# Loading the meta tokens turned: sixteen four-byte-element transfers in place of sixteen TensorE transposes

## The chip, the core and the metric

One core of one Trainium2 chip runs the whole program. The metric is the device time of one execution in microseconds. Before the change it is 2454.93 us (median of three runs, 2454.27 to 2454.93).

## What is computed

The program takes x (256 tokens by D = 2048 features, fp32) through two blocks. The first is an attention block and a squared-ReLU MLP. The second puts 16 learned meta tokens ahead of the 256 tokens, so its first products run over 272 columns:

```python
meta = jnp.broadcast_to(meta_tokens[None].astype(x.dtype), (b, N_META, D_MODEL))   # (1, 16, 2048)
h = jnp.concatenate([meta, x], axis=1)
hn = rms_norm_2(h, norm_mix_g)       # x * rsqrt(mean(x*x)) * gain, per token
proj = hn @ w_in                     # columns of the pool, the convolution and the gates
```

Pool and convolution look back over up to 15 tokens, which is why the meta tokens matter. They are left out again at the end: `return out[:, N_META:]`.

## The kernel before, in words

**Layout.** Activations stand turned: features on the 128 partitions, 16 tiles of 128 features (NT = 16), tokens along the free axis. `a_buf` has 272 columns a tile: 16 for the meta tokens, 256 for x.

**Weights.** All weights are fp32 in HBM and come in chunks of 512 rows by 512 columns (1 MB), over 450 of them. A chunk goes into one of four `raw` buffers by one transfer on SyncE's queue (SP, line 548), which waits until VectorE has split the chunk that stood there. ScalarE rounds each half of a chunk (a unit, [128, 2, 512]) to `whi` (line 602), VectorE takes the rest into `wlo` (line 810), and TensorE multiplies whi by the high and low part of the activations (line 1365 or 1420) and wlo by the high part (line 1372 or 1428). There are four unit buffers of whi and wlo, that is two chunks: ScalarE fills one as soon as TensorE has done with it.

**Stages.** A list of stages is run by every engine in the same order. `q` is chunks 0 to 15, `kv` 16 to 47, `w_o` 48 to 63, and `w1_0`, the first panel stage of the MLP, chunks 64 to 79; then come `w2_0`, `w1_1`, `w2_1`, ..., `w1_3`, `w2_3`, then `u`, the first stage that reads the meta columns. Stages of one iteration are unrolled. Each engine's order is what its `body` writes out: ScalarE's splits a chunk two ahead, then does whatever is written for this chunk, then the evacuation of a panel when its last chunk is at hand.

**Meta tokens.** SyncE loads `meta_tok` ([16, 2048], line 526) behind eight small vectors. In stage q, after chunk (1, 1), TensorE turns it by `meta_turn` (line 1340): sixteen transposes into spare columns of PSUM bank 6. VectorE's `meta_operand` copies them to U (line 882), multiplies by the gain of the norm into `meta_f` (line 884), squares (line 888) and reduces to `msum` (line 890). `meta_f` is a view of the tile rr1, and `msum` of rr, so the trace names them rr1 and rr. Behind stage w1_3 ScalarE's `meta_high` rounds meta_f into the meta columns of a_buf (line 770) and VectorE's `meta_low` takes the rest (line 896). VectorE's `z_out`, in the attention, waits for the reduction, since its tile t2 lies over U.

**The end.** TensorE's last products of the output are those of `last_chunks` (lines 1530 and 1535). VectorE and ScalarE then add, square, scale and store the two halves of the tokens. After `run`, TensorE has 42 products more, called `spare` (line 1605), that nothing reads.

Of the kernel before, what the change touches and what calls it, by code (L numbers as in the profile page):

```python
# [15 lines left out]
ALU = mybir.AluOpType  # L16
# [4 lines left out]
P = 128  # L21
D = 2048
NT = D // P
T = 256
MT = T // P
M = 16
# [235 lines left out]
def build(nc, x, meta, norm_mix, norm_mlp, final_norm, w_qkv, w_o1, w1, w2, norm_mix_2, w_in, b_gate,  # L262
# [6 lines left out]
    with ExitStack() as ctx:  # L269
# [13 lines left out]
        def sem(name):  # L283
            return ctx.enter_context(nc.semaphore(name))
# [46 lines left out]
        sqt = S2[:, :, 0:T]  # L331

        x_tok, _ = place("x_tok", [P, MT, D], at=region)
        meta_tok, _ = place("meta_tok", [M, D], at=region + 16384)
        x_sq, _ = place("x_sq", [P, MT, D], at=b_off)
        gm, _ = place("gm", [NT, P], at=region + 24576 + 1536)
        gv, _ = place("gv", [96, 2, P], at=region + 24576)
# [46 lines left out]
        vec_t = sem("vec_t")  # L384
        vec_ready = sem("vec_ready")
        tr_done = sem("tr_done")
        meta_t = sem("meta_t")
        meta_step = sem("meta_step")
        meta_hi = sem("meta_hi")
        norm_mm = sem("norm_mm")  # L390
# [110 lines left out]
        def _(sp):  # L501
# [16 lines left out]
            def load_vectors():  # L518

                for v, r0 in ((norm_mix[0], V_MIX), (norm_mlp[0], V_MLP), (final_norm, V_FIN1), (norm_mix_2, V_MIX2), (norm_ffn_2, V_FFN2),  # L520
                              (pool_scale, V_PS)):
                    sp.dma_start(gv[r0:r0 + NT, 0, :], v.rearrange("(t p) -> t p", p=P)).then_inc(vec_landed, 16)
                sp.dma_start(gv[0:2 * NT, 1, :], b_gate.rearrange("(t p) -> t p", p=P)).then_inc(vec_landed, 16)
                sp.dma_start(gv[2 * NT:5 * NT, 1, :], conv_w.rearrange("k (t p) -> (k t) p", p=P)
                             ).then_inc(vec_landed, 16)
                sp.dma_start(meta_tok[:], meta).then_inc(meta_landed, 16)

            load_x(0)

# [58 lines left out]
        def _(act):  # L588
            cnt = Counts()
            act.dma_start(gm[:], norm_mix[0].rearrange("(t p) -> t p", p=P)).then_inc(mix_landed, 16)  # L590

            def split_hi(ahead=AHEAD // UNITS):

# [136 lines left out]
            def body(st, i):  # L730
                for q, (k, c) in enumerate(st.order):
                    p = st.panels[k]
                    first = st.name == "q" and k == 0
                    if not first and not split_early[0]:
                        split_hi()
                    split_early[0] = False
                    cnt.n["chunk"] += 1
                    if st.norm is not None and k == 0 and c == NORM_CHUNK:
                        root(st.norm)
                    if st.name == "dn_2" and k == 3 and c == 0:  # L740

                        act.activation(ms[:, 1, 0:2], ms[:, 0, 0:2], ACT.Sqrt)
                    if st.name == "dn_0" and (k, c) in H_TURNS:
                        h_out(H_TURNS.index((k, c)))
                    for g, step in attn_steps(st, q):
                        if step == 7:
                            weights_hi(g)
                    if c == p.chunks - 1:
                        cross_out(p, k % 2)
                        if attn_over(st, q):  # L750

                            split_hi()
                            split_early[0] = True
                        evac(p, k // 2 if p.kind in ("k", "v") else st.index(i, k))
                        cnt.closed(p)
                    for g, step in attn_steps(st, q):
                        if step == 2:
                            softplus_ln(g)
                        if step == 4:
                            softplus_hi(g)  # L760
                        if step == 6:
                            weights_exp(g)
                        if step == 8:
                            evac(ATTN, g)
                            cnt.event("attn")
# [25 lines left out]
        def _(dve):  # L791
# [85 lines left out]

            def meta_operand():

                meta_raw = U[:, 0, 0:NT * M]  # L880
                dve.wait_ge(meta_t, 1)
                dve.tensor_copy(meta_raw, ps[:, 6, T:T + NT * M]).then_inc(meta_step, 1)
                dve.wait_ge(meta_step, 1)
                dve.tensor_tensor(meta_f, meta_raw.rearrange("p (t n) -> p t n", n=M),
                                  vec[:, V_MIX2:V_MIX2 + NT].unsqueeze(2).to_broadcast([P, NT, M]),
                                  ALU.mult).then_inc(meta_step, 1)
                dve.wait_ge(meta_step, 2)
                dve.tensor_tensor(U[:, 1, 0:NT * M], meta_raw, meta_raw, ALU.mult).then_inc(meta_step, 1)
                dve.wait_ge(meta_step, 3)
                dve.tensor_reduce(msum, U[:, 1, 0:NT * M].rearrange("p (t n) -> p n t", n=M), mybir.AxisListType.X,  # L890
                                  ALU.add).then_inc(meta_step, 1)

            def meta_low():

                dve.wait_ge(meta_hi, 1)
                dve.tensor_tensor(a_lo[:, :, 0:M], meta_f, cast(a_hi[:, :, 0:M]), ALU.subtract).then_inc(meta_step, 1)

            def z_out(g):

                dve.wait_ge(z_ready, g + 1)  # L900
                dve.wait_ge(meta_step, 4)
                if g > 0:
                    dve.wait_ge(aw_lo, g)
                for b, hd in ((2, 0), (6, 2)):
# [244 lines left out]
            def body(st, i):  # L1149
                for q, (k, c) in enumerate(st.order):  # L1150
# [9 lines left out]
                    cnt.n["chunk"] += 1  # L1160
                    if st.name == "q" and k == 1 and c == 2:
                        vectors()
                        meta_operand()
                    if st.norm is not None and k == 0 and c == NORM_CHUNK:
                        norm(st.norm)
                    if p.kind == "last" and c == 0:
# [131 lines left out]
        def _(pe):  # L1298
# [28 lines left out]
            def vectors():  # L1327

                pe.wait_ge(vec_landed, 16 * 8)
                pe.wait_ge(diag_ready, 2)  # L1330
                for b, v0, v1 in ((0, 0, V_BG), (1, V_BG, V_END)):
                    last = pe.transpose(ps[:, 7, T + v0:T + v1], gv[0:v1 - v0, b, :], ident[0:v1 - v0, 0:v1 - v0])
                last.then_inc(vec_t, 1)

            def meta_turn():

                pe.wait_ge(meta_landed, 16)
                pe.wait_ge(x_out, PIECES)
                for t in range(NT):
                    last = pe.transpose(ps[:, 6, T + t * M:T + (t + 1) * M], meta_tok[:, t * P:(t + 1) * P],  # L1340
                                        ident[0:M, 0:M])
                last.then_inc(meta_t, 1)

            def token_rows():

# [147 lines left out]
            def norm(k):  # L1493

                pe.wait_ge(sums_ready, k + 1)
                last = pe.matmul(ps[:, 7, 0:T], ones[:], acc[:, 0, :], start=True, stop=True, skip_group_check=True)
                if k == 1:
                    pe.wait_ge(meta_step, 5)
                    pe.matmul(ps[:, 6, 0:M], ones[:], msum, start=True, stop=True, skip_group_check=True)
                    last = pe.matmul(ps[:, 6, M:TW], ones[:], acc2[:, 0, :], start=False, stop=True,  # L1500
                                     skip_group_check=True)
                last.then_inc(norm_mm, 1)
# [53 lines left out]
            def body(st, i):  # L1556
                for q, (k, c) in enumerate(st.order):
# [5 lines left out]
                    if c == 0:  # L1563
# [1 line left out]
                        if st.name == "q" and k == 1:  # L1565
                            pe.wait_ge(vec_ready, 1)
                        if st.name == "u" and k == 0:
                            pe.wait_ge(meta_step, 5)
                        if st.norm == 1 and k == 1:
                            pe.wait_ge(norm_mid, 3)  # L1570
                        elif st.norm is not None and k == 1:
# [6 lines left out]
                        token_rows()  # L1578
                    if st.name == "q" and k == 1 and c == 1:
                        vectors()  # L1580
                        meta_turn()
                    if st.name == "dn_0" and (k, c) in H_TURNS:
                        if (k, c) == H_TURNS[0]:
                            gated[0] = cnt.n["full"]
# [13 lines left out]

            run(pe, cnt, body)

            row = d_hi.rearrange("p t n -> p (t n)")

            def spare(i, stationary, moving, n):

                pe.matmul(ps[:, 2 + i % 2, 0:n], stationary, moving, start=True, stop=True, skip_group_check=True)  # L1605

            def block(i):

                return whi[:, i // 8, i // 4 % 2, i % 4 * P:(i % 4 + 1) * P]

            for i in range(6):
                spare(i, block(0), by_turns(d_hi[:, i, :]), T)
            for i in range(6):
                spare(i, block(i), by_turns(d_hi[:, i, 0:192]), 192)
            for i in range(6):
                spare(i, block(i), by_turns(d_hi[:, i, 0:P]), P)
            for i in range(6):
                spare(i, block(i), row[:, i * T:(i + 8) * T].rearrange("p (a n) -> p n a", a=2)[:, 0:P, :], T)
            for i in range(6):
                spare(i, block(i), d_hi[:, i, :].rearrange("p (a n) -> p n a", a=4), T)  # L1620
            for i in range(6):
                spare(i, block(i), d_hi[:, i, 0:1].to_broadcast([P, T]), T)
            for i in range(6):
                spare(i, b_hi[:, i, 0:P], by_turns(d_hi[:, i, :]), T)


# [21 lines left out]
```

## Time and profile before

| | |
|---|---|
| median of 3 runs | 2454.93 us (2454.27 to 2454.93) |
| the profiled execution's own time | 2454.94 us |
| its span, first to last instruction | 2453.2 us |
| TensorE busy | 2448.2 us |
| VectorE, ScalarE, GpSimd busy | 1652.5, 1206.5, 142.7 us |
| DMA | 485.34 MB, mean 198 GB/s |
| granted TensorE clock | 1.00 throughout |

The span is 1.7 us shorter than the time of the same execution; what lies around the span is not in the trace. Queue q1 is SyncE's, q10 ScalarE's. A packet is one contiguous run of a transfer, or the four-byte write of a semaphore at an engine's end of a transfer. A share of a queue is of 16 engines' time. The chain of work is followed back from the last instruction of an engine, which here isn't the last thing to happen: the stores land after it.

### The profile page before, as it was taken

What the parts mean: (1) busy time and instruction counts of PE and PEld (TensorE: products, weight loads), DVE (VectorE), ACT (ScalarE), POOL (GpSimd) and SP (SyncE); (2) the same over time, 40 slices, a digit from 0 to 9 for tenths busy, and PEclk for the clock granted to TensorE, in tenths of its full rate; (3) what the DMA queues carried; (4) which work ended last, traced back from release to release, by engine and by line L of the source; (5) the groups of instructions that cost most, each with busy time, mean ns of one, the idle gap of its engine ahead of it and who ended that gap; (6) DMA issues with size and microseconds to landing.
All of it is one profiled execution on the core that took longest, in us unless ns stands there. A gap on an engine that the chain in (4) does not pass through costs nothing.

```text
span 2453.2 us, 39643 instructions
## 1 busy us (share of the span) xinstructions
PE 2448.2 (100%) x15839; PEld 2273.1 (93%) x15839; DVE 1652.5 (67%) x1415; ACT 1206.5 (49%) x1185; POOL 142.7 (6%) x87
## 2 busy tenths in 40 slices
PE   9999999999999999999999999999999999999999
PEld 9999999999999999999999999999999889988998
DVE  7677777656656666787765886666766556665665
ACT  5456555444444444544543344544554544444444
POOL 0001100000000000000200630000000000000001
DMA  8655556666666666565656566666666565666664
GB/s 267 200 174 170 172 189 202 196 203 205 196 199 205 199 198 203 190 204 190 205 191 203 191 201 196 203 206 200 195 205 201 192 200 196 204 204 200 197 221 138
DMA packets 243960, 485.34 MB, mean 198 GB/s; under 512 B 7728, under 2 KB 8944, under 8 KB 243696
## 3 DMA queue, kind: packets, MB, share of 16 engines
q1 hardware_dynamic: 243520, 483.12, 59.9%
q8 instruction: 86, 1.41, 0.2%
q10 hardware_dynamic: 320, 0.53, 0.1%
q14 instruction: 34, 0.28, 0.0%
HBM read 481.53 MB, written 2.10 MB: 197 GB/s over the span
## 4 chain that ended last, share of the span: by engine, by line
PE 99%; DMA 0%; issue 0%; DVE 0%; SPq 0%; ACT 0%
PE ps L1365 44%; PE ps L1372 23%; PE ps L1420 12%; PE ps L1399 8%; PE ps L1428 6%; PE ps L1405 4%; PE ps L1476 0%; PE ps L1442 0%; PE ps L1530 0%; DMA raw<-in_sb_w_qkv_dram 0%; PE ps L1464 0%; PE ps L1605 0%; PE ps L1513 0%; PE ps L1535 0%; PE ps L1467 0%
## 5 line engine op out<-in xcount | busy, mean ns | idle before, releaser
L810 DVE TENSOR_TENSOR wlo<-raw,whi 128x1024 fp32r<-128x1024 f32 x900 | 1144.8, 1284 | 750.7 <-ACT whi L602 749.3
L602 ACT ACTIVATE whi<-raw 128x1024 fp32r<-128x1024 f32 x900 | 947.8, 1056 | 1154.1 <-PE ps L1372 815.7
L1365 PE MATMUL ps<-b_buf,whi 128*128 128x512 f32 x2816 | 666.3, 379 | 0.0
L1365 PEld LDWEIGHTS ps<-b_buf,whi 128*128 128x128 f32 x2816 | 506.3, 190 | 56.6
L1372 PEld LDWEIGHTS ps<-b_buf,wlo 128*128 128x128 f32 x2816 | 369.0, 191 | 18.9
L1372 PE MATMUL ps<-b_buf,wlo 128*128 128x256 f32 x2816 | 371.1, 275 | 0.0
L1365 PE MATMUL ps<-c_buf,whi 128*128 128x512 f32 x1280 | 303.0, 380 | 0.0
L1420 PE MATMUL ps<-a_buf,whi 128*128 128x258 f32 (+4 forms) x2304 | 282.2, 276 | 1.1 <-issue 1.1
L1420 PEld LDWEIGHTS ps<-a_buf,whi 128*128 128x128 f32 x2304 | 269.6, 191 | 1.6 <-issue 1.3
L1365 PEld LDWEIGHTS ps<-c_buf,whi 128*128 128x128 f32 x1280 | 230.1, 190 | 25.7
L1365 PE MATMUL ps<-a_buf,whi 128*128 128x512 f32 x896 | 211.9, 379 | 0.0
L1365 PEld LDWEIGHTS ps<-a_buf,whi 128*128 128x128 f32 x896 | 161.0, 190 | 18.0
L1372 PEld LDWEIGHTS ps<-c_buf,wlo 128*128 128x128 f32 x1280 | 167.8, 191 | 8.6
L1372 PE MATMUL ps<-c_buf,wlo 128*128 128x256 f32 x1280 | 168.7, 275 | 0.0
L1399 PE MATMUL ps<-whi,d_buf 128*128 128x512 f32 x672 | 159.1, 380 | 0.0
L1428 PE MATMUL ps<-a_buf,wlo 128*128 128x258 f32 (+4 forms) x1152 | 153.0, 276 | 0.1
L1399 PEld LDWEIGHTS ps<-whi,d_buf 128*128 128x128 f32 x672 | 126.5, 189 | 17.7
L1428 PEld LDWEIGHTS ps<-a_buf,wlo 128*128 128x128 f32 x1152 | 140.3, 191 | 0.4 <-DVE wlo L837 0.3
L1372 PEld LDWEIGHTS ps<-a_buf,wlo 128*128 128x128 f32 x896 | 117.4, 191 | 6.0
L1372 PE MATMUL ps<-a_buf,wlo 128*128 128x256 f32 x896 | 118.1, 275 | 0.0
L985 DVE TENSOR_TENSOR full<-ps,full 128x1024 f32<-128x1024 f32 x78 | 95.0, 1217 | 0.0
L1405 PE MATMUL ps<-wlo,d_buf 128*128 128x512 f32 x336 | 86.2, 379 | 0.0
(204 smaller groups left out, 1374.6 us busy)
## 6 DMA issues: line engine op xcount, KB each, us to landing
raw<-in_mlp_w_dram SPq DMA_DIRECT2D x128, 1024.0 KB, 5.2
raw<-in_w_in_dram SPq DMA_DIRECT2D x96, 1024.0 KB, 5.1
raw<-in_w_gate_up_dram SPq DMA_DIRECT2D x88, 1024.0 KB, 5.0
raw<-in_sb_w_qkv_dram SPq DMA_DIRECT2D x44, 1024.0 KB, 5.1
raw<-in_w_down_dram SPq DMA_DIRECT2D x44, 1024.0 KB, 5.1
raw<-in_sb_w_o_dram SPq DMA_DIRECT2D x16, 1024.0 KB, 5.2
raw<-in_conv_out_w_dram SPq DMA_DIRECT2D x16, 1024.0 KB, 5.1
raw<-in_w_o_dram SPq DMA_DIRECT2D x16, 1024.0 KB, 5.1
```

Of the source, the lines that this page charges most:

```text
L602: act.activation(whi[:, unit_of(n, u)], raw[:, n % RAW, u * UK:(u + 1) * UK, :], ACT.Copy).then_inc(w_hi, 1)
L810: dve.tensor_tensor(wlo[:, s], raw[:, n % RAW, u * UK:(u + 1) * UK, :], cast(whi[:, s]), ALU.subtract).then_inc(w_lo, 1)
L985: step(dve.tensor_tensor(in_halves(full[:]), turned(half, 0), in_halves(full[:]), ALU.add))
L1365: pe.matmul(ps[:, 4 * half + j, :].rearrange("p (c n a) -> p c n a", c=2, a=2), whi[:, unit_of(n, u), kt, j * P:(j + 1) * P], parts_by_tur ...
L1372: last = pe.matmul(ps[:, 4 * half + j, T:2 * T], wlo[:, unit_of(n, u), kt, j * P:(j + 1) * P], by_turns(buf[:, 0, p.tile0 + c * KT + u * U ...
L1399: pe.matmul(ps[:, 4 * half + m, :], part[:, x, toks[m]], by_turns(whi[:, s, kt, :]), start=first and kt == 0 and part is hi, stop=False, s ...
L1405: last = pe.matmul(ps[:, 4 * half + m, :], hi[:, x, toks[m]], by_turns(wlo[:, s, kt, :]), start=False, stop=stop and kt == UK - 1, skip_gr ...
L1420: pe.matmul(outs[j], whi[:, s, kt, j * P:(j + 1) * P], by_turns(part[:, x, tok]), start=first and kt == 0 and part is hi and (wide_ or j % ...
L1428: last = pe.matmul(outs[j], wlo[:, s, kt, j * P:(j + 1) * P], by_turns(hi[:, x, tok]), start=False, stop=stop and kt == UK - 1, skip_group ...
```

## The change

SyncE no longer loads meta_tok. In stage w1_0 ScalarE issues, once for each of the 16 chunks, a transfer that reads 128 features of the 16 meta tokens from HBM turned, straight into meta_f: 128 partitions by 16 elements, each element a run of four bytes of its own. TensorE's sixteen transposes and VectorE's copy out of PSUM are gone. VectorE's three other operations on them move from stage q to behind stage w1_3, right ahead of meta_low, and ScalarE's meta_high now waits for them there. z_out's wait goes. The wait for x_out moves from meta_turn into `vectors`. The 42 spare products are gone too.

```diff
-                sp.dma_start(meta_tok[:], meta).then_inc(meta_landed, 16)
@@ scalar
+            def load_meta(t):
+
+                act.dma_start(meta_f[:, t, :], meta[:, t * P:(t + 1) * P].rearrange("m p -> p m"),
+                              allow_slow_non_contiguous=True).then_inc(meta_landed, 16)
@@ scalar, body: behind split_hi() and the count of the chunk
+                    if st.name == "w1_0":
+                        load_meta(q)
@@ vector
             def meta_operand():
-                meta_raw = U[:, 0, 0:NT * M]
-                dve.wait_ge(meta_t, 1)
-                dve.tensor_copy(meta_raw, ps[:, 6, T:T + NT * M]).then_inc(meta_step, 1)
+                squares = U[:, 1, 0:NT * M]
+                dve.wait_ge(meta_landed, 16 * NT)
+                dve.tensor_tensor(squares, rr1[:], rr1[:], ALU.mult).then_inc(meta_step, 1)
                 dve.wait_ge(meta_step, 1)
-                dve.tensor_tensor(meta_f, meta_raw.rearrange("p (t n) -> p t n", n=M),
-                                  vec[:, V_MIX2:V_MIX2 + NT].unsqueeze(2).to_broadcast([P, NT, M]),
+                dve.tensor_tensor(meta_f, meta_f, vec[:, V_MIX2:V_MIX2 + NT].unsqueeze(2).to_broadcast([P, NT, M]),
                                   ALU.mult).then_inc(meta_step, 1)
-                dve.wait_ge(meta_step, 2)
-                dve.tensor_tensor(U[:, 1, 0:NT * M], meta_raw, meta_raw, ALU.mult).then_inc(meta_step, 1)
-                dve.wait_ge(meta_step, 3)
-                dve.tensor_reduce(msum, U[:, 1, 0:NT * M].rearrange("p (t n) -> p n t", n=M), mybir.AxisListType.X,
+                dve.tensor_reduce(msum, squares.rearrange("p (t n) -> p n t", n=M), mybir.AxisListType.X,
                                   ALU.add).then_inc(meta_step, 1)
             def meta_low():
+                meta_operand()
                 dve.wait_ge(meta_hi, 1)
@@ vector, z_out
-                dve.wait_ge(meta_step, 4)
@@ vector, body, stage q
                         vectors()
-                        meta_operand()
@@ tensor, vectors
+                pe.wait_ge(x_out, PIECES)
@@ tensor
-            def meta_turn():
-
-                pe.wait_ge(meta_landed, 16)
-                pe.wait_ge(x_out, PIECES)
-                for t in range(NT):
-                    last = pe.transpose(ps[:, 6, T + t * M:T + (t + 1) * M], meta_tok[:, t * P:(t + 1) * P],
-                                        ident[0:M, 0:M])
-                last.then_inc(meta_t, 1)
@@ tensor, behind run(pe, cnt, body): seven groups of six products into banks 2 and 3, all gone
-            for i in range(6):
-                spare(i, block(0), by_turns(d_hi[:, i, :]), T)
...
-            for i in range(6):
-                spare(i, b_hi[:, i, 0:P], by_turns(d_hi[:, i, :]), T)
```

In `norm` and ahead of stage u TensorE waits for meta_step 4 in place of 5, one step fewer having been made.

## Rows read from the trace of the kernel before

**Rows 1.** The page: the span, and busy time of each engine.
```profile
span 2453.2 us, 39643 instructions
PE 2448.2 (100%) x15839; PEld 2273.1 (93%) x15839; DVE 1652.5 (67%) x1415; ACT 1206.5 (49%) x1185; POOL 142.7 (6%) x87
```

**Rows 2.** Busy time in stretches: stage w1_0, w2_0, start, middle, end.
```profile
core 0: us, PE busy (x) PEld busy (x) DVE busy (x) ACT busy (x) POOL busy (x), PEclk, DMA share, GB/s
380.40:464.80 84.40, 84.40 (x517) 77.48 (x517) 61.40 (x54) 43.81 (x43) 1.84 (x2) 1.00 0.63 200
464.80:548.60 83.80, 83.80 (x514) 76.93 (x513) 50.50 (x43) 38.43 (x37) 0.00 (x0) 1.00 0.61 201
...
13.90:2446.00 2432.10, 2430.84 (x15721) 2256.68 (x15721) 1642.15 (x1400) 1197.82 (x1173) 140.93 (x77) 1.00 0.60 197
```

**Rows 3.** The chain in order of time, around the transposes: start, us, what.
```profile
43.22 0.89 PE ps L1428 x8
44.12 0.16 PE ps L1332 x2
44.27 1.09 PE ps L1340 x16
45.36 1.98 PE ps L1420 x16
47.34 0.89 PE ps L1428 x8
48.23 1.79 PE ps L1420 x16
```

**Rows 4.** Timeline of the end.
```profile
2446.00 4.37 PE L1605 MATMUL ps<-d_buf,whi 128*128 128x256 f32 x36
...
2448.67 0.75 DVE L1088 TENSOR_SCALAR y_tok<-y_tok,stat 128x1024 f32<-128x1024 f32 x1
...
2450.20 0.83 PE L1605 MATMUL ps<-d_buf,b_buf 128*128 128x256 f32 x6
```

**Rows 5.** What SyncE's own queue waited for, from 2435 us on.
```profile
SPq L269 <- DMA out_dram<-y_tok: 3.0, 1, 3.0
SPq L269 <- PEq L269: 0.2, 1, 0.2
```

**Rows 6.** DMA from 384 to 464 us: packets, queue, weight loads.
```profile
q1 hardware_dynamic: 7955, 15.80, 62.8%
raw<-in_mlp_w_dram SPq DMA_DIRECT2D x15, 1024.0 KB, 5.3
```

**Rows 7.** Queues from 2.5 to 5 us, then from 4 to 6 us.
```profile
q10 hardware_dynamic: 14, 0.00, 0.7%
...
q1 hardware_dynamic: 540, 0.65, 98.3%
```

**Rows 8.** Timelines: a weight load's issue, ScalarE's splits, TensorE's first products of w1_0.
```profile
356.88 5.61 SPq L548 DMA_DIRECT2D raw<-in_mlp_w_dram  x2
...
372.94 1.06 ACT L602 ACTIVATE whi<-raw 128x1024 fp32r<-128x1024 f32 x1 [1.62 <-PE ps L1372]
...
380.54 1.89 PE L1365 MATMUL ps<-c_buf,whi 128*128 128x512 f32 x8
```

**Rows 9.** Issue of a transfer: SyncE's of meta_tok, and line 548's on the weights.
```profile
15.69 0.42 SPq L526 DMA_DIRECT2D meta_tok<-in_meta_tokens_dram  x1
L548 SPq DMA_DIRECT2D raw<-in_mlp_w_dram x128: 367/373/393, 356.9 to 1025.7; - x128
```

**Rows 10.** Timeline of VectorE in stage q.
```profile
53.55 0.42 DVE L882 COPY U<-ps 128x256 f32<-128x256 f32 x1
54.01 0.42 DVE L884 TENSOR_TENSOR rr<-U,vec 128x256 f32<-128x256 f32 x1
54.47 0.43 DVE L888 TENSOR_TENSOR U<-U 128x256 f32<-128x256 f32 x1
54.93 0.59 DVE L890 TENSOR_REDUCE rr<-U 128x16 f32<-128x256 f32 x1
```

**Rows 11.** Timeline behind stage w1_3.
```profile
975.20 0.40 ACT L770 ACTIVATE a_buf<-rr 128x256 fp32r<-128x256 f32 x1
...
976.21 1.22 DVE L1110 TENSOR_TENSOR b_buf<-full,b_buf 128x1024 f32 x1
```

More of the change, by code:

```diff
@@ L333, in build @@
         x_tok, _ = place("x_tok", [P, MT, D], at=region)
-        meta_tok, _ = place("meta_tok", [M, D], at=region + 16384)
         x_sq, _ = place("x_sq", [P, MT, D], at=b_off)
@@ L386, in build @@
         tr_done = sem("tr_done")
-        meta_t = sem("meta_t")
         meta_step = sem("meta_step")
@@ L1497, in norm @@
                 if k == 1:
-                    pe.wait_ge(meta_step, 5)
+                    pe.wait_ge(meta_step, 4)
                     pe.matmul(ps[:, 6, 0:M], ones[:], msum, start=True, stop=True, skip_group_check=True)
@@ L1567, in body @@
                         if st.name == "u" and k == 0:
-                            pe.wait_ge(meta_step, 5)
+                            pe.wait_ge(meta_step, 4)
                         if st.norm == 1 and k == 1:
@@ L1580, in body @@
                         vectors()
-                        meta_turn()
                     if st.name == "dn_0" and (k, c) in H_TURNS:
@@ L1599, in _ @@
             run(pe, cnt, body)
[L1601 to L1609, printed above, removed]
-            for i in range(6):
-                spare(i, block(0), by_turns(d_hi[:, i, :]), T)
-            for i in range(6):
[L1614 to L1623, printed above, removed]
-                spare(i, b_hi[:, i, 0:P], by_turns(d_hi[:, i, :]), T)
 _INS = ["x", "meta_tokens_2", "norm_mix", "norm_mlp", "final_norm", "sb_w_qkv", "sb_w_o", "mlp_w1", "mlp_w2",
```

## The prediction, made before the changed kernel was run

> **What bounds the kernel now.** I read the page's busy times first: TensorE is busy for 2448.2 of 2453.2 us, the next engine, VectorE, for 1652.5 [rows 1]. The table of stretches then shows that nearly all of the missing time lies outside the middle: from 13.9 to 2446.0 us TensorE is busy for 2430.84 of 2432.10 us, at full clock, and in the two MLP stages that the change touches first it isn't idle at all [rows 2]. So TensorE sets the time between the first chunk and the last, and whatever another engine or a transfer does counts only where it makes TensorE wait. The chain of waits in order of time shows what one step of it costs; the end I read from the timeline and from SyncE's waits, because there the chain of the page follows the wrong thing (below).
>
> **TensorE loses sixteen transposes.** They stand on the chain itself, 1.09 us from 44.27 to 45.36, with no wait ahead or behind [rows 3]. The next sixteen products take 1.98 us where the same ones later take 1.79 [rows 3]; that 0.19 us comes with the change of product and may stay, because the two transposes of the vectors remain ahead of them. So the gain here is 1.09 to 1.28 us. I take 1.2. It is passed on to the end: the weights are split for TensorE well ahead of need (worked out below), so nothing is late next. The wait for x_out that moves into `vectors` is for copies of the first panel, whose results the products of that panel have used; TensorE reaches it three chunks later, at 44 us: nothing.
>
> **TensorE loses 42 products at the end.** They run from 2446.00 to 2451.03 [rows 4]. But the last scaling of the output ends at 2448.67 + 0.75 = 2449.42 [rows 4], its store is issued after it, and SyncE then waits 3.0 us for the stores to land, and only 0.2 us for TensorE's queue [rows 5]. With 0.4 us for the issue, 2449.8 + 3.0 is 2452.8, which is later than 2451.03 by 1.8 us and leaves the span's end at 2453.2. The products lie beside the tail, so I cost them at nothing. If that cover were gone, the price would be at most what they last, 4.9 us.
>
> **VectorE.** One copy (0.42 us) goes, and three operations of 0.43, 0.42 and 0.59 us move [rows 10]. They leave a stage where TensorE waited for nothing, so their going gives nothing. Behind w1_3 they are new work on a path: ScalarE's meta_high ran at 975.20, because its operand had been ready since 54 us, while VectorE took the low part of the last panel from 976.21 to 977.43 [rows 11]. Now meta_high must wait for that, for the squares and for the product with the gain: 977.43 + 0.43 + 0.42 + some 0.1 = 978.4 us, and it ends at 978.8. The split that is queued behind it on ScalarE came at 975.91 in the trace and now comes 2.9 us later. VectorE's own split, queued behind meta_operand and meta_low, ends about 2.2 us later. TensorE needs that split's unit three units on. A unit is half of a chunk, and the second stretch has 16 chunks in 83.80 us, so a chunk is 5.24 us and a unit 2.62 [rows 2]. ScalarE's split takes 1.06 us [rows 8], so it has 3 x 2.62 - 1.06 = 6.8 us to spare. 2.9 us fit in, and are made up within three units. Cost: nothing; if ScalarE had no such lead it would be 2.9 us.
>
> **ScalarE issues sixteen transfers.** The trace has an issue at 0.42 us for a small pattern and at 0.37 for a full 1 MB load [rows 9], so the number of packets doesn't show in it. ScalarE is busy for 43.81 us of the 84.40 of w1_0 [rows 2], 2.7 of each chunk's 5.24 us; 0.42 more leaves 2.1 us idle. One issue stands ahead of the norm's root at chunk 2 and delays it by at most 0.4 us; TensorE has the rest of the panel until it needs the scale's work. SyncE loses one issue of 0.42 us and 128 KB of traffic at a time when no weight is late: nothing. What could cost here is an issue that doesn't return until its packets are taken; that is a rival.
>
> **The transfers themselves** are the one term that could be large. Each has 128 x 16 = 2048 runs of four bytes: on each of 16 engines 128 packets and one for the semaphore, 129. The stage's own load: 7955 packets took 62.8% of 16 engines for 80 us, which is 101 ns a packet; a 1 MB chunk is 33 packets an engine, 3.3 us in every 5.24 [rows 6]. So 1.9 us a chunk are free on every engine. The trace of before has no read of four bytes. Its nearest row from below is the ScalarE queue at the start, where 14 packets of 512 bytes or of four (semaphores) took 0.7% of 16 engines for 2.5 us: 20 ns each [rows 7]. Its next is the stretch from 4 to 6 us, mostly runs of 1 KB: 540 packets in 98.3% of 32 us, 58 ns [rows 7]. The far end is the 101 ns of the 2 KB packets. I take 20 ns, since a four-byte packet is nearest to that row in size and the three rows fall with size. It gives 129 x 20 = 2.6 us a chunk, which is 0.7 more than is free. Served ahead of the weights throughout, that makes them late by 16 x 0.7 = 11 us at the end of the stage. Against it stands a lead: the load of chunk 64 is issued at 356.88 and lands 5.3 us later, at 362.2, and ScalarE first reads it at 372.94, so 10.8 us to spare; with the 6.8 of the split buffers, TensorE doesn't see a weight that is up to 17.6 us late [rows 6, 8]. 11 is less than 17.6: hidden, and with 0 ns a packet all the more. The landing itself has 500 us until it is needed.
>
> **The sum.** Against the profiled execution: 2454.94 - 1.2 = 2453.7 us, of which 2452.0 would be its span. That execution stands 0.01 us from the median, so the forecast for the median is 2453.7 too. No measurement of this kernel tells a change under 0.2% (4.9 us) from none with safety, so this is "within 0.2%".
>
> **Rivals.**
> (a) *The small packets are served in runs ahead of the weights, and each costs more than I take.* Engine time is then simply added. The stage's lateness is 16 x (129c - 1.9 us), and TensorE sees what passes 17.6 us: it decides from c = 23 ns on, little above what I take. At 58 ns: 16 x (7.5 - 1.9) = 89, less 17.6, is 72 us, 2526 us; at 101 ns 2614. For it: a run of four bytes has a read in HBM of its own, and no row shows one. Against it: packet time falls with size in all rows. Of the Trainium skill, "DMA: Bandwidth & Descriptors", section "Queues, rings and completion order", states that an engine changes between queues only after a whole group of typically 9 to 17 descriptors; by that rule this is how the queues would share, where one for one would be rival (b). The trace has no stretch in which both queues are full, so it doesn't show which. The same page's "Rules for kernel authors" says that turning data by a rearranged access pattern is a bad way to do it, 19 times slower than the transposing transfer; no row here bears on that factor, and it would speak for (a).
> (b) *The queues take turns packet by packet, and a four-byte packet costs as much as a weight's.* Weights then go at 101 + c ns a packet until the 16 x 129 = 2064 small ones of an engine are through. In that time 2064 / 33 = 62.5 chunks pass, which TensorE would use up in 328 us; with the lead of 17.6 it decides from c = 66 ns on. At 101 ns: 2064 x 0.202 = 417, less 345, is 72 us, 2526 us again. It needs a packet at the far bound.
> (c) *The issue blocks ScalarE until its transfer is taken.* Were each as long as a weight load's landing, 5.3 us, ScalarE would need 2.7 + 5.3 = 8.0 us a chunk for 5.24: 16 x 2.8 = 44, less its lead of 6.8, is 38 us, 2493 us. It decides from an issue of about 2.95 us on. Against it: 0.37 us for a load of 512 packets [rows 9].
> (d) *The change doesn't gain what it removes*: the time of the transposes is taken by a wait of TensorE's at that place or later. 2454.9 us. Against it: ScalarE's and VectorE's leads.
> (e) *The 42 products do set the end*, their modelled ends being too early. At most 4.9 + 1.2 less: 2448.8 us. Against it: SyncE's 3.0 us of waiting for the store.
>
> **How the numbers follow.** Hidden as forecast 0.69, (d) 0.06, (a) 0.11, (b) 0.07, (c) 0.05, (e) 0.02. The two first are within 0.2%: same 0.75. (a), (b) and (c) are slower: 0.23, save that each starts small beyond its threshold. (e) is faster: 0.02. The range goes from 2452.6 (1.28 us of gain, and half a microsecond and more of the runs' own scatter with a little of the tail) to 2463, which takes in (d) and the part of (a) to (c) just above their thresholds, c up to 27 ns in (a) (16 x 129 x 4 ns = 8 us), some 0.05. About 0.2 is left out, almost all of it above.
>
> **What would show it.** In the profile after: TensorE's products follow the two transposes of the vectors directly, and TensorE has no idle time from 380 to 560 us that the weights end. ScalarE's queue should have some 33,000 packets at about 20 ns; a share of q10 above 3 us a chunk, or weight loads of w1_0 that land in more than 15 us, would mean (a) or (b), and then VectorE's and ScalarE's idle time would end with a transfer. An issue above 1 us on ScalarE's queue would mean (c). TensorE should be idle in the last 7 us while the span's end stays 7 us behind the last product. meta_high should come 3 us later, with no gap on TensorE. The prediction is wrong if a four-byte packet costs more than 23 ns and is served first.

## The result, and the profile after

The changed kernel takes 2515.97 us (median of six runs, 2508.30 to 2520.47) against 2454.93 us before: a ratio of 1.0247, 95% interval 1.0237 to 1.0258. The forecast was 2453.7 us and no measurable change; the range ended at 2463. The profiled execution took 2513.46 us, its span is 2511.7, 58.5 us more than before.

The page of the changed kernel, its first parts (compare [rows 1]; the slices of the clock and of the GB/s are 63 us each):

```profile
span 2511.7 us, 39538 instructions
PE 2459.5 (98%) x15781; PEld 2276.5 (91%) x15781; DVE 1651.9 (66%) x1414; ACT 1204.7 (48%) x1185; POOL 142.4 (6%) x87
PEclk9999999889999999999999999999999999999999
GB/s 270 201 168 168 184 185 128 118 163 200 200 201 202 199 202 199 199 188 199 200 201 201 187 199 201 201 201 201 201 201 200 197 200 199 200 201 206 201 217 137
q10 hardware_dynamic: 33344, 0.66, 0.7%
```

TensorE has 58 fewer products and is busy for 11 us more. The rate drops in slices 7 to 9 (377 to 565 us), which hold stage w1_0 and the start of w2_0, and the clock stands at 8 tenths in slices 8 and 9. ScalarE's queue has the 33,000 packets foreseen, and they took even less than foreseen by the record: 0.7% of 16 engines for 2511.7 us is about 8.4 ns each. By that number alone they would be free.

Stretches of the changed kernel, the same columns as in [rows 2]:

```profile
440.00:460.00 20.00, 9.82 (x45) 8.26 (x44) 4.75 (x4) 4.92 (x5) 0.00 (x0) 0.76 0.42 113
...
380.00:560.00 180.00, 138.29 (x737) 120.65 (x736) 84.59 (x73) 59.31 (x60) 1.84 (x2) 0.89 0.47 133
560.00:980.00 420.00, 420.00 (x2566) 385.67 (x2565) 261.02 (x218) 196.62 (x190) 0.00 (x0) 1.00 0.62 201
```

And the stretch from 380 to 560 us of the kernel before:

```profile
380.00:560.00 180.00, 180.00 (x1102) 165.25 (x1100) 119.47 (x102) 88.05 (x86) 1.84 (x2) 1.00 0.62 201
```

That closes the account. Before, a product took 180.00 / 1102 = 163 ns here. The changed kernel's 737 would take 120.4 us at that rate and took 138.29: 17.9 us are the slower clock. 180 - 138.3 = 41.7 us are idle. Together 59.6, and 58.5 + 1.2 of gain at the start is 59.7. Nothing is lost anywhere else: from 560 to 980 us TensorE is never idle, over the moved steps behind w1_3 too.

What TensorE waited for, in the whole changed kernel (total, times, longest), then what ScalarE waited for from 380 to 600 us:

```profile
PE ps L1356 <- ACT whi L604: 39.0, 12, 5.9
PE ps L1363 <- DVE wlo L814: 2.6, 4, 1.2
...
ACT whi L604 <- issue: 52.3, 8, 9.4
ACT full L661 <- issue: 26.0, 4, 8.8
```

TensorE waits for ScalarE's splits, and ScalarE waits for "issue": for its own stream, not for a weight. The weights do come slower: from 380 to 540 us a load lands in 12.3 us (median; 15.6 at most) in place of 5.3 [rows 6], but no wait of ScalarE's ends with one. Its timeline names the instruction:

```profile
385.48 0.41 ACTq L591 DMA_DIRECT2D rr<-in_meta_tokens_dram  x1
...
389.96 0.38 ACTq L591 DMA_DIRECT2D rr<-in_meta_tokens_dram  x1
...
395.20 8.44 ACTq L591 DMA_DIRECT2D rr<-in_meta_tokens_dram  x1
403.66 1.28 ACT L698 ACT_TABLE_LOAD   x1 [7.42 <-issue]
403.84 9.67 ACTq L591 DMA_DIRECT2D rr<-in_meta_tokens_dram  x1
...
434.41 11.07 ACTq L591 DMA_DIRECT2D rr<-in_meta_tokens_dram  x1
435.33 1.04 ACT L604 ACTIVATE whi<-raw 128x1024 fp32r<-128x1024 f32 x1
445.58 1.06 ACT L604 ACTIVATE whi<-raw 128x1024 fp32r<-128x1024 f32 x1 [9.22 <-issue]
```

Line 591 is load_meta. The first two issues take 0.4 us, as [rows 9] had it; from the third on ScalarE stands still for 2.7 to 11.2 us at each. And TensorE's products behind such a wait run slower; the eight of whi take 1.89 us where nothing is late, as the third row shows:

```profile
446.78 3.73 PE L1356 MATMUL ps<-c_buf,whi 128*128 128x512 f32 x8 [5.74 <-ACT whi L604]
450.33 1.07 PE L1363 MATMUL ps<-c_buf,wlo 128*128 128x256 f32 x8
451.24 1.89 PE L1356 MATMUL ps<-c_buf,whi 128*128 128x512 f32 x8
```

The mean granted clock of 440 to 460 us is 0.76 of full, between the two levels of 1.2 and 2.4 GHz: after an idle 5.7 us the engine came back at the lower one, and it had the full one again some 4 us later.

### The profile page after: what moved, and what is told of

It is laid out like the page before. It is cut to its first block, busy times and chain, and to the rows that moved or that the text cites. A ratio compares the mean times of both kernels' runs of the same rounds, so it can differ in the third digit from the quotient of the medians.

```text
span 2511.7 us, 39538 instructions
## 1 busy us (share of the span) xinstructions
PE 2459.5 (98%) x15781; PEld 2276.5 (91%) x15781; DVE 1651.9 (66%) x1414; ACT 1204.7 (48%) x1185; POOL 142.4 (6%) x87
## 4 chain that ended last, share of the span: by engine, by line
PE 94%; issue 3%; ACTq 1%; ACT 1%; DVE 1%; DMA 0%; SPq 0%; DVEq 0%
PE ps L1356 41%; PE ps L1363 21%; PE ps L1411 12%; PE ps L1390 8%; PE ps L1419 6%; PE ps L1396 4%; ACTq L591 1%; ACT whi L604 0%; PE ps L1467 0%; PE ps L1433 0%; DMA raw<-in_sb_w_qkv_dram 0%; PE ps L1521 0%; PE ps L1455 0%; DVE full L1009 0%; DVE full L985 0%
## 5 line engine op out<-in xcount | busy, mean ns | idle before, releaser
L1356 PE MATMUL ps<-c_buf,whi 128*128 128x512 f32 x1280 | 313.9, 389 | 29.8 <-ACT whi L604 29.8
L1356 PEld LDWEIGHTS ps<-c_buf,whi 128*128 128x128 f32 x1280 | 236.5, 195 | 59.3 <-issue 31.3
L661 ACT ACTIVATE full<-ps 128x1024 f32<-128x1024 f32 x78 | 78.9, 1012 | 26.0 <-issue 26.0
```

Of the source, the lines that this page charges most:

```text
L661: act.activation(in_halves(full[:]), turned(half, 1), ACT.Copy).then_inc(act_done, 1)
L1356: pe.matmul(ps[:, 4 * half + j, :].rearrange("p (c n a) -> p c n a", c=2, a=2), whi[:, unit_of(n, u), kt, j * P:(j + 1) * P], parts_by_tur ...
```

## The experiments

Each kernel is the changed one with a short edit, unless it says otherwise. All were compared with the kernel before on the same chip, whose medians there were 2454.79 to 2454.82 us.

### Is it ScalarE's blocked stream, or the weights that come late?

Two theories were on record: the queue's own pace blocks ScalarE (Q), or the small packets crowd out the weights (W).

**e_every2**: 2458.48 us (2453.21 to 2462.29), ratio 1.0013 (1.0004 to 1.0022).

```diff
-                    if st.name == "w1_0":
-                        load_meta(q)
+                    n_at = cnt.n["chunk"] - 1 - 48 if st.name in ("kv", "w_o", "w1_0") else -1
+                    if n_at >= 0 and n_at % 2 == 0:
+                        load_meta(n_at // 2)
```

> The same sixteen transfers of 2048 four-byte runs on ScalarE's queue, but one at every second chunk of w_o and w1_0 (10.5 us apart) in place of one at every chunk of w1_0 (5.24 us apart). Theory Q (the queue takes a transfer in some 8.6 us, holds about two, and a third blocks ScalarE's instruction stream until there is room; the weights' own lateness plays no part): 8.6 is less than 10.5, so every issue is about 0.4 us, TensorE waits nowhere, 2453.7 us. Theory W (the small packets crowd the weights out of the DMA engines: a transfer costs the weights 8.6 us of the engines' time): two chunks leave 3.8 us free, so the weights fall behind by 16 x 4.8 = 77 us, less 17.6 of lead: about 2513 us, with waits that end with a weight load.

Between the theories, nearer to Q. At 10.5 us a transfer TensorE waits 1.0 us in the profile, whose execution took 2456.28 us; what the slower executions lost isn't in it. W's sum, in which engine time is simply added, is some 55 us too high. But Q had every issue at 0.4 us, and nine of the sixteen still take 1.8 to 9.8; three of ScalarE's waits end with one. Seven more end with a weight that is late, which Q had left out:

```profile
ACT whi L604 <- issue: 16.7, 3, 8.8
ACT whi L604 <- DMA raw<-in_mlp_w_dram: 9.9, 5, 3.8
ACT whi L604 <- DMA raw<-in_sb_w_o_dram: 6.5, 2, 4.0
```

**e_every4**: the same edit with 16 and 4 for 48 and 2. 2453.61 us (2453.27 to 2454.58), ratio 0.9996 (0.9987 to 1.0005).

> One transfer at every fourth chunk from chunk 16 to chunk 76 (21 us apart), all else as in the change. Theory Q: every issue about 0.4 us and 2453.7 us, the 1.2 us of the transposes gained. Theory W: four chunks leave 7.6 us free, 1.0 less than a transfer takes, 16 us of lateness in all, within the lead of 17.6: also 2453.7. If it comes to 2454.9 or more, then what moved behind stage w1_3 costs what the transposes had cost.

As both theories had it. This is what the prediction had expected of the change itself: the same transfers and the same moved steps, 1.2 us less than before. Every issue takes 0.37 to 0.41 us.

**e_gpsimd** gives the transfers to GpSimd's queue, one a chunk of w1_0, held to the pace by a wait for w_hi. ScalarE issues none. 2507.79 us (2506.63 to 2512.26), ratio 1.0222 (1.0206 to 1.0237).

```diff
+                    if st.name == "w1_0":
+                        pool.wait_ge(w_hi, cnt.n["chunk"] * UNITS)
+                        pool.dma_start(meta_f[:, q, :], meta[:, q * P:(q + 1) * P].rearrange("m p -> p m"),
+                                       allow_slow_non_contiguous=True).then_inc(meta_landed, 16)
```

> The same sixteen transfers, one a chunk of w1_0, but issued by GpSimd, which has nothing else to do there; ScalarE issues none. Theory Q (what is lost is ScalarE's time, blocked by its own issues, and the slower TensorE clock behind the waits that this makes): TensorE waits nowhere in w1_0, 2453.7 us. Theory W (the small packets make the weights late whoever issues them): 2500 us or more, with ScalarE's waits ended by weight loads.

**Theory Q fell here.** ScalarE is free, and nearly the whole loss stays. Waits of TensorE (whole kernel) and ScalarE (380 to 600 us), and the queues from 440 to 460 us:

```profile
PE ps L1358 <- ACT whi L604: 40.0, 6, 11.0
...
ACT whi L604 <- DMA raw<-in_mlp_w_dram: 94.2, 12, 16.0
...
q0 software_dynamic: 120, 0.02, 44.5%
q1 hardware_dynamic: 1413, 2.81, 40.0%
```

Now the weights come late, up to 16 us each. So the blocked stream isn't the cause but one of two ways in which it shows: in the change the queue pushes back on ScalarE, ScalarE splits later, and weights are then asked for so slowly that none is late.

**e_two_queues**: ScalarE issues the even transfers, SyncE the odd ones, ahead of that chunk's weights. 2489.78 us (two runs, 2484.91 and 2494.66), ratio 1.0143 (1.0124 to 1.0161).

```diff
-                    if st.name == "w1_0":
+                    if st.name == "w1_0" and q % 2 == 0:
                         load_meta(q)
@@ sync, ahead of the weight load
+                    if st.name == "w1_0" and n % 2 == 1:
+                        t = n - 64
+                        sp.dma_start(meta_f[:, t, :], meta[:, t * P:(t + 1) * P].rearrange("m p -> p m"),
+                                     allow_slow_non_contiguous=True).then_inc(meta_landed, 16)
```

> Still one transfer a chunk of w1_0, but ScalarE and SyncE issue them in turns, each one in 10.5 us. If the 8.6 us are a limit of each queue: no issue blocks, 2453.7 us. If they are a limit that both queues share (16 x 8.6 = 138 us of work for 84 us of stage): both block as before, and as SyncE's blocks the weight loads too, 2490 to 2530 us.

The limit is shared by the queues: some 26 us better than the change, at the lower edge of what a shared limit was expected to give. ScalarE's longest issue is 9.0 us, SyncE's 5.6, and ScalarE waits 61.1 us for late weights. The Trainium skill, "DMA: Bandwidth & Descriptors", section "Issuing engines are not separate DMA queues", has this: whoever issues, the same 16 engines do the work. Three issuers here (ScalarE, SyncE, GpSimd) agree with it.

**e_burst**: transfers in bursts of 1, 2, 3, 4 and 6 at chunks 16, 24, 32, 40 and 48. 2511.83 us, one run.

```diff
+                    first_of = {16: (0, 1), 24: (1, 2), 32: (3, 3), 40: (6, 4), 48: (10, 6)}
+                    if st.name in ("kv", "w_o") and cnt.n["chunk"] - 1 in first_of:
+                        t0, many = first_of[cnt.n["chunk"] - 1]
+                        for t in range(t0, t0 + many):
+                            load_meta(t)
```

> Bursts of 1, 2, 3, 4 and 6 transfers on ScalarE's queue, at chunks 16, 24, 32, 40 and 48, 42 us apart. Theory Q: first and second issue of a burst about 0.4 us each, from the third on 8 us or so each; ScalarE has 6.8 us of lead, so the bursts of 3, 4 and 6 cost TensorE some 2, 10 and 27 us. If an issue's time goes by its own pattern, not by what stands in the queue, all are alike.

A miss in its detail. A burst of two already takes 6.1 us of ScalarE's stream, not 0.8; the one of four 22.8:

```profile
147.86 6.11 ACTq L591 DMA_DIRECT2D rr<-in_meta_tokens_dram  x2
...
257.15 5.61 ACTq L591 DMA_DIRECT2D rr<-in_meta_tokens_dram  x2
262.79 17.20 ACTq L591 DMA_DIRECT2D rr<-in_meta_tokens_dram  x2
```

So the queue holds more than one such transfer and less than two. The cost came to 57 us, not 39. These bursts meet the attention: TensorE's three waits there (47.8 us) end with VectorE's part of the weights of the softmax, and VectorE had waited 48.1 us for ScalarE's, which stood behind the issues. What makes up the other 9 us wasn't followed.

### What is it in a transfer that takes so long?

**e_run8**: 1024 runs of eight bytes each. 2453.67 us. **e_run64**: 128 runs of 64 bytes. 2453.58 us (ratio 0.9996, 0.9986 to 1.0005). **e_half4**: 1024 runs of four bytes; only eight of the sixteen meta tokens are loaded turned, the tile being filled by one contiguous transfer before. 2453.32 us. In the first two the meta columns hold other values than the reference's, in the third half of them.

The theories in the next expectations: by L every four-byte run has its price, so their number counts; by S runs under eight bytes are dear; by H the distance of the sources in HBM costs. C and P, further on, are two forms of H: crowding of all engines' reads into the same few hundred bytes, and the pitch of 8 KB between an engine's successive reads.

```diff
# e_run8
+                act.dma_start(meta_f[:, t, :].rearrange("p (m two) -> p m two", two=2),
+                              meta[0:8, t % 8 * 2 * P:(t % 8 + 1) * 2 * P].rearrange("m (p two) -> p m two", two=2),
# e_run64
+                act.dma_start(meta_f[:, t, :], meta[t, :].rearrange("(p m) -> p m", m=M),
# e_half4 (the contiguous load that fills the tile before isn't shown)
+                act.dma_start(meta_f[:, t, 0:8], meta[0:8, t * P:(t + 1) * P].rearrange("m p -> p m"),
```

> Each transfer reads and writes 1024 runs of eight bytes in place of 2048 of four, same bytes, same places in the program (the values in the meta columns are then not the reference's). Theory Q with a price for each run (8.6 us / 2048 = 4.2 ns): 4.3 us a transfer, less than the 5.24 of a chunk, no blocking issue, 2453.7 us. If the price goes by bytes or by transfer, it stays near 2513 us.

> Each transfer reads one row of the meta tokens as 128 contiguous runs of 64 bytes, same bytes and same issues (the values in the meta columns are then not the reference's). Both theories Q and W, by the count of runs: 2453.7 us, issues of 0.4 us. If an issue is slow because it stands in that place of ScalarE's stream, or the moved steps behind w1_3 cost time, it stays above: up to 2513 us by the first, 2454.9 by the second.

> One transfer a chunk of w1_0 as in the change, each of 1024 four-byte runs (half of the meta tokens' values aren't loaded turned). Theory L: half of a transfer's cost, some 6.3 us by the profile's pause or 3.3 by the lateness, against 2.4 free in a chunk: 16 x 0.9 to 3.9 late, less 17.6: 2453.7 to 2500 us. Theory S (four bytes are dear): near the upper end. If only the number of runs counts, as in the kernel with 1024 runs of eight bytes: 2453.7.

All three cost nothing and keep the 1.2 us, so neither the place of the issues, nor their number, nor the bytes matter. Half the runs are enough to hide everything, though three of e_half4's issues take 1.6 to 2.2 us.

**e_near4**: 2048 runs of four bytes again, but read side by side from one row, and written 8 bytes apart (other values than the reference's). 2453.29 us (2452.74 to 2453.75), ratio 0.9993 (0.9982 to 1.0004).

```diff
+                act.dma_start(meta_f[:, t // 2 * 2:t // 2 * 2 + 2, :].rearrange("p a m -> p (a m)").rearrange(
+                              "p (m two) -> p m two", two=2)[:, :, t % 2], meta[t, :].rearrange("(p m) -> p m", m=M),
```

> One transfer a chunk of w1_0, 2048 four-byte runs each, sources side by side in one row of 8 KB (the values in the meta columns are then not the reference's). Theory L: as the change, about 2514 us. Theory H (the sources' distance in HBM is what costs): 2453.7 us.

Theory L fell, and with it the count of runs as the cause: as many packets, as small, at the same places, and they land in 3.5 us (median) in place of 23.8. e_near4 differs from the change in where it reads and in where it writes. The form 64p + 8192m of the table below settles which: it writes as the change does and is as fast. What matters is where in HBM they read.

**e_alone** and **e_alone2** are e_every4 with eight transfers behind the last store, each awaited before the next; their own times (2501.84 and 2505.14 us) are longer by these.

```diff
+            for i, (dst, src) in enumerate(forms):
+                act.dma_start(dst, src, allow_slow_non_contiguous=True).then_inc(alone, 16)
+                act.wait_ge(alone, 16 * (i + 1))
# a few of the forms (e_alone2); the 1 MB load beside the last one, issued by SyncE, isn't shown
+                turned4 = (meta_f[:, 0, :], meta[:, 0:P].rearrange("m p -> p m")),
+                (meta_f[:, :, 0], meta[0, :].rearrange("(t p) -> p t", p=P)),
+                (column, meta.rearrange("m (p q) -> p m q", q=16)[:, :, 0]),
+                (column, w_gate_up[0:M, 0:P].rearrange("m p -> p m")),
```

> The kernel of one transfer at every fourth chunk, and behind its last store eight transfers on ScalarE's queue, each awaited before the next, with nothing else on the DMA engines: the turned one of 2048 four-byte runs; 1024 four-byte runs; 1024 eight-byte runs; 2048 four-byte runs whose sources lie side by side; 2048 whose sources lie 64 bytes apart; 128 runs of 64 bytes; a 1 MB weight block; and the turned one again with a 1 MB load issued by SyncE at the same moment. The kernel's time itself is longer by these. Theory L (a four-byte run holds its engine for some 98 ns, seen between 177 and 182 us, whatever stands beside it, and the record shows only 8 of them): 129 x 98 ns = 12.6 us and 2 us of fixed cost for the turned one, half of it for 1024 runs, and the 1 MB load beside it takes 5 us + up to 12. Theory H (the distance of the sources in HBM, 8 KB, makes it): the side-by-side form lands in 4 us or less. Theory S (runs under eight bytes are dear, not their number): 1024 runs of four bytes take 7 us or more, of eight bytes 4.5.

> Behind the last store eight transfers of 2048 four-byte runs (the seventh: 128 runs of 64 bytes), each awaited before the next, nothing beside the first seven. Sources by partition p and element m: (1) 4p + 8192m bytes, the change's; (2) 4p + 512m; (3) 64p + 8192m; (4) 4p + 45056m, in another tensor; (5) 16p + 8192m; (6) 8p + 8192m; (8) the change's again, with a 1 MB load on SyncE's queue issued some 4 us behind it. Theory C (crowding: the sixteen engines at one time read the same 512 bytes of HBM): 1, 2 and 4 take some 75 ns a packet and engine, 6 half of it, 5 a quarter, 3 the 11 of the side-by-side form. Theory P (the 8 KB pitch of an engine's successive reads): 1, 3, 5 and 6 at 75, 2 and 4 at 11 to 20. For 8: a weight load issued with a turned transfer took 6.0 us against 5.1 alone; if one that comes behind it in time lands in 10 us or more, small reads already under way hold it up.

The time to landing is the list of issues' of the trace. The last column is worked out from the records of the packets: from the start of a transfer's first to the start of its last, by the packets of an engine (129, or 65 for the half ones).

| source of element m of partition p, bytes | packets | landing, us | ns a packet and engine |
|---|---|---|---|
| 4p + 8192m, the change's | 2064 | 11.1 (both kernels) | 75 (both) |
| 4p + 8192m, eight m only | 1040 | 6.3 | 75 |
| 8p + 8192m, runs of eight bytes | 1040 | 4.1 | 43 |
| 8p + 8192m | 2064 | 8.9 | 59 |
| 16p + 8192m | 2064 | 4.4 | 23 |
| 64p + 8192m | 2064 | 2.9 | 11 |
| 4p + 45056m, another tensor | 2064 | 3.4 | 16 |
| 4p + 512m, one meta token | 2064 | 2.7 | 10 |
| 64p + 4m, side by side | 2064 | 3.3 | 11 |
| 1024p + 64m | 2064 | 3.1 | 12 |

Three of these rows as e_alone2's lists of issues have them, for 4p + 512m, 16p + 8192m and 8p + 8192m:

```profile
rr<-in_meta_tokens_dram ACTq DMA_DIRECT2D x1, 8.0 KB, 2.7
...
rr<-in_meta_tokens_dram ACTq DMA_DIRECT2D x1, 8.0 KB, 4.4
...
rr<-in_meta_tokens_dram ACTq DMA_DIRECT2D x1, 8.0 KB, 8.9
```

And e_alone from 2451.4 us on, with the change's form by itself in 40 slices of 0.29 us: 2064 packets trickle for 33 of the slices, the engines are busy for nearly nothing, and it takes 11.1 us to land.

```profile
DMA  0000000000000000000000000000000000001000
GB/s 0 0 0 0 1 1 1 1 1 1 1 1 1 1 1 1 1 1 1 1 1 1 1 1 1 1 1 1 1 1 1 1 1 1 1 1 1 0 0 0
q10 hardware_dynamic: 2064, 0.01, 7.8%
rr<-in_meta_tokens_dram ACTq DMA_DIRECT2D x1, 8.0 KB, 11.1
```

Neither theory holds by itself. Crowding (all engines in the same 512 bytes at one time) had 4p + 512m slow, and it is the fastest; the pitch of 8 KB had 64p + 8192m slow, and it isn't. It takes both: sources of neighbouring partitions within 4 to 16 bytes of each other, the dearer the closer, and successive reads 8 KB on. What it is about 8 KB stays open: pitches of 45056 bytes (in another tensor) and of 512 cost 16 and 10 ns, and no others were tried with neighbours four bytes apart.

The last transfer of each kernel has a 1 MB load beside it. Issued together, the load took 6.0 us, where one alone took 5.1, and the turned transfer 13.5 in place of 11.1. Issued 4.8 us behind it (e_alone2, at 2491.73 us; both on SyncE's queue), the load took 11.3. From 2486.5 to 2501 us, in 40 slices of 0.36:

```profile
GB/s 1 0 0 0 1 1 1 1 1 1 1 1 1 1 1 1 1 1 1 1 1 1 1 1 1 1 0 0 0 1 12 51 147 271 339 350 379 384 367 266
raw<-in_w_down_dram SPq DMA_DIRECT2D x1, 1024.0 KB, 11.3
rr<-in_meta_tokens_dram ACTq DMA_DIRECT2D x1, 8.0 KB, 13.6
```

The load is asked for in slice 15 and moves next to nothing up to slice 30, by whose end (2497.4 us) nine tenths of the small packets have gone. So small reads under way hold up a load that comes behind them. e_every4 shows the same in the running kernel, from 177 to 182 us: the weights' queue moves next to nothing while a transfer's packets trickle, 812 / 16 = 51 an engine in 5 us, 98 ns each. The load that was asked for at 173.89 us, 3.4 behind the transfer, lands after 15.0 us.

```profile
q10 hardware_dynamic: 812, 0.00, 7.2%
q1 hardware_dynamic: 34, 0.07, 4.5%
```

### The version that follows

**e_token** is the change with its sixteen transfers cut by token, not by tile. The same bytes, runs and places, and the kernel computes the reference: 2453.56 us (2453.37 to 2454.20), ratio 0.9995 (0.9985 to 1.0005).

```diff
-                act.dma_start(meta_f[:, t, :], meta[:, t * P:(t + 1) * P].rearrange("m p -> p m"),
+                act.dma_start(meta_f[:, :, t], meta[t, :].rearrange("(t p) -> p t", p=P),
```

> The change with its sixteen transfers cut the other way: each takes one meta token (one row of 8 KB in HBM) for all sixteen tiles, still 2048 four-byte runs and one transfer a chunk of w1_0. Theory P: 2453.5 us, no issue above 0.6 us. Theory C: as the change, 2508 to 2520 us.

As theory P had it, though P as a whole didn't stand. From 384 to 464 us:

```profile
q1 hardware_dynamic: 8070, 16.04, 64.0%
q10 hardware_dynamic: 30960, 0.12, 21.6%
raw<-in_mlp_w_dram SPq DMA_DIRECT2D x15, 1024.0 KB, 5.5
rr<-in_meta_tokens_dram ACTq DMA_DIRECT2D x16, 8.0 KB, 3.4
```

The weights land in 5.5 us, as before in 5.3 [rows 6]; the small packets take 8.9 ns of an engine each, and this time they cost no more than they show. TensorE is never idle from 380 to 460 us. Its ten runs lie wholly below the thirteen of the kernel before (2454.35 to 2455.55), though the interval of the ratio takes in 1: 1.3 us is at the edge of what can be measured here.

### The 42 products at the end

**e_no_spare** is the kernel before without them (`for i in range(6): spare(...)`, seven times, taken out): 2454.60 us (2454.16 to 2455.52) against 2454.82, ratio 0.9999 (0.9990 to 1.0008).

> The kernel before without its 42 unread products at the end, nothing else. Prediction: the stores set the end, 2454.9 us. Rival: TensorE's queue sets it, up to 2450 us.

They hid behind the stores. Rival (e) is out.

## Why the prediction was wrong

**The step that failed is the price of a four-byte packet.** "I take 20 ns, since a four-byte packet is nearest to that row in size and the three rows fall with size" [rows 7]. The record of a packet is short indeed (8.4 ns), but it isn't what the packet costs: with the change's sources each holds its engine for 75 ns alone, within my bounds of 20 and 101, and near the far one. The quantity that the rows were ordered by was also the wrong one: at the same size and number, 10 to 75 ns come out by where the sources lie. The rows that I had, semaphores and whole rows of vectors, said nothing of reads 8 KB apart. With no row for that, the far end should have stood in the range, all the more since the decision point of rival (a) was 23 ns, only 3 above the value that I took. One of the signs that I set was blind for the same reason: by the record q10's share is 129 x 8.4 ns = 1.1 us a chunk, far below the 3 us that would have meant (a) or (b).

**Which rival it was.** The price and the decision were (a)'s, the form was (c)'s. (c) asked for an issue of more than 2.95 us, and they take 2.7 to 11.2; "the number of packets doesn't show" in an issue is true only while the queue has room, which is gone with the second transfer. As an independent rival (c) was mispriced: the issue blocks because the transfer is slow, and e_run8 and e_near4, with the same issues, block nowhere. (a)'s sum, engine time simply added, would give 16 x (129 x 0.075 - 1.9) - 17.6 = 107 us late; 41.7 were idle. For e_half4, with 65 packets, it would give 30 us, and nothing was lost. The two kinds of packet overlap in part, as the 13.5 us for 11.1 and 5.1 show, and a blocked ScalarE asks for fewer weights. (b), packets in turn, decides only from 66 ns, which 75 passes, and its sum at 75 ns is 2064 x 0.176 - 345 = 18 us, too little. A load issued behind a turned transfer took 11.3 us and not the 6.0 of one issued with it, so the queues don't simply alternate either. What the exact sharing is stays open. (The 2493 us written with (c) leave out the 1.2 of gain; its own sum is 2492.)

The groups of 9 to 17 descriptors of the Trainium skill, "DMA: Bandwidth & Descriptors", section "Queues, rings and completion order", which were cited with (a), no run here shows. They were also put to the wrong rival: queues that are served in turn, group by group, share on average as in (b), and nothing in that rule puts the small packets ahead. The rule of the Trainium skill's same page, section "Rules for kernel authors", against turning by a rearranged access pattern pointed the right way, but e_token turns by such a pattern too and costs nothing.

**The clock was left out.** I priced lateness alone; 17.9 of the 59.6 us are products at the lower clock behind TensorE's waits.

**What held.** The transposes: TensorE's chain in the changed kernel has the two transposes of the vectors, and the group behind them takes 1.83 us in place of 1.98 [rows 3], so 1.24 us are gained against 1.2 forecast; every kernel with the sixteen transfers in which they don't hold TensorE up came to 2453.3 to 2453.7 us.

```profile
44.30 0.16 PE ps L1332 x2
44.46 1.83 PE ps L1411 x16
```

The moved steps cost nothing: in e_token meta_high runs at 976.73 us, 10.4 us behind TensorE's first product of that chunk's b_buf where before it was 7.4 behind, which is the 3 us foreseen [rows 11], and TensorE goes on without a gap. The first row is the kernel before's:

```profile
967.85 1.89 PE L1365 MATMUL ps<-b_buf,whi 128*128 128x512 f32 x8
...
966.32 1.89 PE L1356 MATMUL ps<-b_buf,whi 128*128 128x512 f32 x8
...
976.27 0.42 DVE L888 TENSOR_TENSOR rr<-rr,vec 128x256 f32<-128x256 f32 x1
976.73 0.42 ACT L774 ACTIVATE a_buf<-rr 128x256 fp32r<-128x256 f32 x1 [2.96 <-DVE rr L888]
```

The end held too, by e_no_spare.

## What to carry to other kernels

A packet's recorded time is not its price: a transfer of small runs can take 11 us with its engines "busy" for 8% of them, so price it by its landing when alone, and compare that with the interval at which it is issued. Where a transfer must have runs of four bytes, try a cut whose reads stay within one row; here, with rows of 8 KB, the same bytes turned by token land in 3.4 us and turned by tile in 23.8. And an engine that feeds the bound one shouldn't issue transfers whose queue may be full, for the issue then blocks its whole stream. But moving the issue alone cures little: from GpSimd the same transfers still cost 53 us, for the weights then came late.

## What wasn't expected of the hardware

- A four-byte read from HBM costs its DMA engine 10 to 75 ns by the addresses alone; of the forms tried, those with neighbouring partitions 4 to 16 bytes apart and a pitch of 8 KB are slow (75 to 23 ns), the others take 10 to 16. The Trainium skill, "DMA: Bandwidth & Descriptors", section "Latency and other measured facts", tells of slow copies at row pitches of 512 KB and more in powers of two; here 8 KB is enough for reads of four bytes, and at 64 bytes between partitions it makes no difference.
- ScalarE's queue takes between one and two transfers of 2064 packets; after that an issue lasts until there is room, up to 11.2 us in the changed kernel.
- After 5.7 us of waiting TensorE ran its next eight products in 3.73 us in place of 1.89, and had its full speed again behind them.
